# One opening block: the input loaded first, the first norm beside the bias rows' preparation, stores waited for after block 1

## The reference

```python
h = rms_norm(x, attn_norm[i])                 # block 1: x * rsqrt(mean(x*x) + 1e-6) * gain
proj = h @ w_in[i]
...
lam = (exp(sum(lambda_q1 * lambda_k1)) - exp(sum(lambda_q2 * lambda_k2)) + lambda_init)
...
bias = bias_table[:, t5_bucket(rel * dilation)]      # block 3: table (3*16 heads, 32 buckets)
...
bias = rpb[:, :, col_idx][:, row_idx]                # block 4: rpb (16 heads, 15, 31)
```

## Time and profile before

| | us |
|---|---|
| median of 3 runs (lowest, highest) | 1720.3 (1716.7, 1722.6) |
| the profiled execution | 1728.3 |
| its span, first to last instruction | 1726.2 |
| TensorE busy | 1564.6 (91%) |
| VectorE busy | 1074.9 (62%) |
| ScalarE busy | 699.1 (40%) |

### The profile page before, as it was taken

How to read it: one execution, slowest core, us unless ns; L and a number is a source line. 1 busy time by engine, 2 the same in 40 slices (tenths; PEclk the granted TensorE clock), 3 DMA queues, 4 the chain that set the end, 5 groups by cost and what they waited for, 6 DMA issues and landing times. The chain is left out here.

```text
span 1726.2 us, 28966 instructions
## 1 busy us (share of the span) xinstructions
PE 1564.6 (91%) x8809; PEld 1383.0 (80%) x8809; DVE 1074.9 (62%) x2752; ACT 699.1 (40%) x1526; POOL 5.8 (0%) x13
## 2 busy tenths in 40 slices
PE   2997789998998999999999999879999997869987
PEld 1664578887997888999999999779999997658885
DVE  3577457957997776666666666555555554266663
ACT  0343211113323443544444444346555554336552
POOL 0000000000000000000000000000000000000000
PEclk9998789999999999999999999989999999679997
DMA  6410043442224555555555555374444441075410
GB/s 246 164 38 1 2 160 111 153 153 75 92 90 142 194 191 188 194 184 182 194 184 182 194 184 183 127 261 135 151 152 137 134 139 45 1 250 165 121 26 25
DMA packets 162586, 239.33 MB, mean 139 GB/s; under 512 B 41808, under 2 KB 91472, under 8 KB 161488
## 3 DMA queue, kind: packets, MB, share of 16 engines
q1 hardware_dynamic: 162160, 238.34, 42.2%
q10 hardware_dynamic: 352, 0.07, 0.0%
HBM read 237.09 MB, written 1.28 MB: 138 GB/s over the span
## 5 line engine op out<-in xcount | busy, mean ns | idle before, releaser
L187 PE MATMUL experts_acc<-experts_uh,experts_wh 128*128 128x512 f32 x512 | 201.5, 394 | 5.7 <-DVE experts_ul L1579 5.7
L188 PE MATMUL experts_acc<-experts_ul,experts_wh 128*128 128x512 f32 x512 | 201.1, 393 | 0.0
L189 PE MATMUL experts_acc<-experts_uh,experts_wl 128*128 128x512 f32 x512 | 200.1, 391 | 0.0
L1132 PE MATMUL plain_u<-ffn_h,down_raw 128*128 128x256 f32 x832 | 192.1, 382 | 0.4 <-PEq L1217 0.4
L1552 ACT ACTIVATE experts_uh<-ffn_h 128x512 fp32r<-128x512 f32 x256 | 147.1, 624 | 83.7 <-PE experts_acc L189 79.1
L189 PE MATMUL projection<-hT_high,down_low 128*128 128x256 f32 x608 | 172.1, 283 | 0.0
L188 PE MATMUL projection<-hT_low,down_high 128*128 128x256 f32 x608 | 172.0, 283 | 0.0
L187 PE MATMUL projection<-hT_high,down_high 128*128 128x256 f32 x608 | 171.7, 282 | 0.0
L1132 PEld LDWEIGHTS plain_u<-ffn_h,down_raw 128*128 128x128 f32 x832 | 154.1, 192 | 19.5 <-issue 1.1
L1579 DVE TENSOR_TENSOR experts_ul<-ffn_h,experts_uh 128x512 fp32r<-128x512 f32 x256 | 164.7, 684 | 3.0 <-ACT experts_uh L1552 3.0
L187 PE MATMUL mix_a_pj<-mix_a_wh,hT_high 128*128 128x384 f32 x384 | 136.8, 356 | 17.0 <-DVE mix_a_wl L560 17.0
(11 more groups left out here) (274 smaller groups left out, 3014.9 us busy)
## 6 DMA issues: line engine op xcount, KB each, us to landing
down_raw<-in_downT SPq DMA_DIRECT2D x256, 256.0 KB, 3.4
ffn_h<-in_up SPq DMA_DIRECT2D x256, 256.0 KB, 2.8
mix_a_w_raw<-in_wa SPq DMA_DIRECT2D x48, 768.0 KB, 5.9
block_w_raw<-in_w SPq DMA_DIRECT2D x16, 768.0 KB, 6.6
mix_b_w_raw<-in_wb SPq DMA_DIRECT2D x16, 768.0 KB, 6.7
route_raw<-in_route SPq DMA_DIRECT2D x16, 576.0 KB, 3.7
wo<-in_wo SPq DMA_DIRECT2D x2, 2048.0 KB, 10.4
mix_a_w_raw<-in_wa SPq DMA_DIRECT2D x16, 256.0 KB, 3.3
```

Of the source, the lines that this page charges most:

```text
L187: pe.matmul(out, lhs[0], rhs[0], start=start, stop=False, skip_group_check=True)
L188: pe.matmul(out, lhs[0], rhs[1], start=False, stop=False, skip_group_check=True)
L189: return pe.matmul(out, lhs[1], rhs[0], start=False, stop=stop, skip_group_check=True)
L1132: mm = pe.matmul(self.u[b][:, 0:SEQ], self.raw[b][:, k, :], self.h[:, k, :], start=k == 0, stop=k == KD - 1, skip_group_check=True)
```

## The change

`prepare_phase` and the first `norm_phase` become one block, `opening_phase`. SP loads x first, each tile with a semaphore of its own, and the first pair's weights before the band mask; the later pairs' weights follow the constants, and two constants that only later blocks read come last. The first norm's steps are woven into the streams of the preparation: VectorE does the inverse root right after the turned table's copy, TensorE the transposes right after the one-hot product, and the lambda products stand between the second and third eviction. The seven strided copies into `staged` move from VectorE to ScalarE, the zeroing of `staged` to GpSimd. The padded table is no longer gathered in SBUF by 16 loads: SP stores a tile of zeros to `bias_pad`, and, at the start of block 1 and after a wait for that store, copies `rpb` into its place from memory to memory. The waits for the stores and for the two late constants stand at the end of SP's stream of block 1 (`finish`). `staged` and the zeros live through block 1.

```diff
 def attention_phase(nc, name, pieces, *, n_pairs, kinds, groups, hT, yT, cons, q_gain=None, k_gain=None,
-                    bias=None, load_bias=None, near=None, minus_lam=None, ahead=None):
+                    bias=None, load_bias=None, near=None, minus_lam=None, ahead=None, finish=None):
...
                 else:
                     load_piece(0, 0, 2)
                 each_pair(sp, n_pairs, one)
+            if finish is not None:
+                finish(sp)
 
...
-def prepare_phase(nc, d, sbt, scratch, ahead):
-
+def opening_phase(nc, d, sbt, scratch, pieces, gain, whole, staged, zeros, stored, pad_zeroed, late):
...
         rows = sb("rows", [3 * N_HEADS, 2 * SEQ])
-        staged = sb("staged", [3 * N_HEADS, SHIFTS, P])
-        pad = sb("pad", [N_HEADS * REL_ROWS, PAD_C])
         prod = sb("prod", [P, 2, HD])
...
+        x_in = [sem(f"x{t}") for t in range(NT)]
...
         block = c.enter_context(nc.Block())
-        loads = [(sbt[k][:], d[k]) for k in ("x", "columns")]
-        loads += [(sbt["rows"][:], d["rows"].broadcast_to([P, N_ROWS]))]
-        loads += [(sbt[k][:], d["c_" + k]) for k in ("cos", "sin", "causal", "near", "iota")]
 
         @block.sync
         def _(sp):
+            for t in range(NT):
+                sp.dma_start(x[:, t, :], d["x"][:, t, :]).then_inc(x_in[t], 16)
+            sp.dma_start(ident[:], d["c_ident"]).then_inc(ident_in, 16)
             sp.dma_start(table[:], d["t5_bias"]).then_inc(table_in, 16)
-            sp.dma_start(sbt["ident"][:], d["c_ident"]).then_inc(ident_in, 16)
             sp.dma_start(onehot[:], d["c_onehot"]).then_inc(table_in, 16)
+            sp.dma_start(sbt["columns"][:], d["columns"]).then_inc(columns_in, 16)
+            pieces.load(sp, 0, 0, 0)
             sp.dma_start(band[:], d["c_band"]).then_inc(table_in, 16)
-            for dst, src in loads:
-                sp.dma_start(dst, src).then_inc(loaded, 16)
-            ahead(sp)
+            sp.dma_start(sbt["rows"][:], d["rows"].broadcast_to([P, N_ROWS])).then_inc(loaded, 16)
+            for k in ("cos", "sin", "causal"):
+                sp.dma_start(sbt[k][:], d["c_" + k]).then_inc(loaded, 16)
+            for q in range(1, pieces.depth):
+                pieces.load(sp, q, q, 0)
+            for k in ("near", "iota"):
+                sp.dma_start(sbt[k][:], d["c_" + k]).then_inc(late, 16)
+            sp.wait_ge(blanked, 2)
+            sp.dma_start(scratch["pad"].rearrange("h r c -> (h r) c"), zeros[:]).then_inc(pad_zeroed, 16)
             sp.wait_ge(rows_ready, 1)
             sp.dma_start(scratch["rows"], staged[:]).then_inc(stored, 16)
-            sp.wait_ge(stored, 32)
-            sp.wait_ge(loaded, 16 * len(loads))
+            sp.wait_ge(loaded, 64)
+
+        @block.gpsimd
+        def _(pool):
+            pool.memset(staged[:], 0.0).then_inc(blanked, 1)
+            pool.memset(zeros[:], 0.0).then_inc(blanked, 1)
 
         @block.scalar
         def _(act):
-            act.wait_ge(zeroed, 1)
-            for h in range(N_HEADS):
-                act.dma_start(pad[h * REL_ROWS:(h + 1) * REL_ROWS, 48:48 + RPB_C],
-                              d["rpb"][h, 4:4 + REL_ROWS, :]).then_inc(rpb_in, 16)
-            act.wait_ge(rpb_in, 16 * N_HEADS)
-            act.dma_start(scratch["pad"].rearrange("h r c -> (h r) c"), pad[:]).then_inc(stored, 16)
+            act.wait_ge(x_in[1], 16)
+            act.activation(sq[:, 1, :], x[:, 1, :], ACT.Square, accum_out=ssum[:, 1:2]).then_inc(sum_ready, 1)
+            act.wait_ge(root_ready, 1)
+            act.activation(h[:, 1, :], x[:, 1, :], ACT.Copy, scale=r[:, 1:2]).then_inc(h_ready, 1)
             act.wait_ge(lsum_ready, 1)
             act.activation(lexp[:], lsum[:], ACT.Exp).then_inc(lexp_ready, 1)
-
-        @block.gpsimd
-        def _(pool):
-            pool.memset(pad[:], 0.0).then_inc(zeroed, 1)
+            act.wait_ge(blanked, 1)
+            act.wait_ge(rows_banded, 1)
+            for m in range(SHIFTS):
+                last = act.activation(staged[:, m, 0:P - 1], rows[:, m:m + RES * (P - 2) + 1:RES], ACT.Copy)
+            last.then_inc(rows_ready, 1)
 
         @block.tensor
         def _(pe):
             pe.wait_ge(ident_in, 16)
             pe.wait_ge(table_in, 48)
-            pe.transpose(pst[0:T5_BUCKETS, 0:3 * N_HEADS], table[:], sbt["ident"][0:48, 0:48]).then_inc(turned, 1)
+            pe.transpose(pst[0:T5_BUCKETS, 0:3 * N_HEADS], table[:], ident[0:48, 0:48]).then_inc(table_turned, 1)
             pe.wait_ge(tableT_ready, 1)
             pe.matmul(psr[0:3 * N_HEADS, :], tableT[:], onehot[:], start=True, stop=True).then_inc(rows_ps, 1)
+            for t in range(NT):
+                if t == 1:
+                    pe.wait_ge(h_ready, 1)
+                else:
+                    pe.wait_ge(root_ready, 2)
+                for k in range(KD):
+                    mm = pe.transpose(pt[:, 2 * t + k // 4, k % 4, :], h[:, t, k * P:(k + 1) * P], ident[:])
+                    if k % 4 == 3:
+                        mm.then_inc(turned, 1)
 
         @block.vector
         def _(dve):
-            dve.wait_ge(turned, 1)
+            dve.wait_ge(x_in[0], 16)
+            dve.tensor_tensor_reduce(sq[:, 0, :], x[:, 0, :], x[:, 0, :], 1.0, 0.0, ALU.mult, ALU.add, ssum[:, 0:1])
+            dve.drain()
+            dve.wait_ge(table_turned, 1)
             dve.tensor_copy(tableT[:], pst[0:T5_BUCKETS, 0:3 * N_HEADS]).then_inc(tableT_ready, 1)
+            dve.wait_ge(sum_ready, 1)
+            inverse_root(dve, r[:], ssum[:], D, hm[:], a[:], b_[:])
+            dve.tensor_copy(a[:], r[:]).then_inc(root_ready, 1)
+            dve.tensor_scalar(h[:, 0, :], x[:, 0, :], r[:, 0:1], None, ALU.mult).then_inc(root_ready, 1)
             dve.wait_ge(rows_ps, 1)
-            dve.memset(staged[:], 0.0)
-            dve.tensor_tensor(rows[:], psr[0:3 * N_HEADS, :], band[:], ALU.add)
-            dve.drain()
-            for m in range(SHIFTS):
-                last = dve.tensor_copy(staged[:, m, 0:P - 1], rows[:, m:m + RES * (P - 2) + 1:RES])
-            last.then_inc(rows_ready, 1)
-            dve.wait_ge(loaded, 16 * len(loads))
-            g = sbt["rows"]
-            lam0 = 4 * P
-            for i in range(2):
-                o = lam0 + 2 * i * HD
-                dve.tensor_tensor_reduce(prod[:, i, :], g[:, o:o + HD], g[:, o + HD:o + 2 * HD], 1.0, 0.0, ALU.mult,
-                                         ALU.add, lsum[:, i:i + 1])
-            dve.drain()
-
-            dve.tensor_scalar(g[:, 0:P], g[:, 0:P], HD ** -0.5, None, ALU.mult).then_inc(lsum_ready, 1)
-            dve.tensor_scalar(g[:, 2 * P:3 * P], g[:, 2 * P:3 * P], HD ** -0.5, None, ALU.mult)
+            dve.tensor_tensor(rows[:], psr[0:3 * N_HEADS, :], band[:], ALU.add).then_inc(rows_banded, 1)
+
+            dve.wait_ge(columns_in, 16)
+            for n in range(2 * NT):
+                t, k = n // 2, slice(4 * (n % 2), 4 * (n % 2) + 4)
+                dve.wait_ge(turned, n + 1)
+                dve.tensor_tensor(whole[:, k, t * P:(t + 1) * P], pt[:, n, :, :], gain[:, k].unsqueeze(2).broadcast_to([P, 4, P]),
+                                  ALU.mult)
+                if n == 1:
+                    dve.wait_ge(loaded, 64)
+                    g = sbt["rows"]
+                    lam0 = 4 * P
+                    for i in range(2):
+                        o = lam0 + 2 * i * HD
+                        dve.tensor_tensor_reduce(prod[:, i, :], g[:, o:o + HD], g[:, o + HD:o + 2 * HD], 1.0, 0.0, ALU.mult,
+                                                 ALU.add, lsum[:, i:i + 1])
+                    dve.drain()
+
+                    dve.tensor_scalar(g[:, 0:P], g[:, 0:P], HD ** -0.5, None, ALU.mult).then_inc(lsum_ready, 1)
+                    dve.tensor_scalar(g[:, 2 * P:3 * P], g[:, 2 * P:3 * P], HD ** -0.5, None, ALU.mult)
             cols = sbt["columns"]
             for k, n in (("q_a", 3), ("q_b", 1)):
...
-
-            def load_first(sp):
-                for q in range(pieces.depth):
-                    pieces.load(sp, q, q, 0)
-            prepare_phase(nc, d, sbt, scratch, load_first if start < 1 else lambda sp: None)
+            staged, zeros = sb("staged", [3 * N_HEADS, SHIFTS, P], c=c), sb("zeros", [N_HEADS * REL_ROWS, PAD_C], c=c)
+            stored, pad_zeroed, late = sem("bias_stored"), sem("pad_zeroed"), sem("late")
             if start < 1:
                 whole = sb("block1_h", [P, KD, SEQ], c=c)
-                norm_phase(nc, "norm0", x, column("attn", KD), None, sbt["ident"], whole=whole)
+                opening_phase(nc, d, sbt, scratch, pieces, column("attn", KD), whole, staged, zeros, stored, pad_zeroed, late)
                 yT = [sb(f"yT0_{n}", [P, KD, SEQ], F32R, c=c) for n in ("high", "low")]
                 wo, landed, load_wo = output_weights(c, "wo1", d["wo1"])
+
+                def store_pad(sp):
+                    load_wo(sp)
+                    sp.wait_ge(pad_zeroed, 16)
```

(34 more changed lines are left out.)

## The result

The changed kernel took 1707.8 us (1707.4 to 1711.5, four runs) against 1720.4 beside it: a ratio of 0.9934, 95% interval 0.9914 to 0.9954. That is 11 us less, between 8 and 15, or 12.7 by the medians. The forecast was 17.3. The direction and the mechanism held; the gain was a quarter to a third smaller than forecast, and the forecast's 0.990 lies outside the interval. Three executions of the later experiments took 2027 to 4023 us, with both forms of the kernel, and the medians and ratios here leave them out.

What follows compares the result with a forecast made beforehand. A 13 us hole behind a late store was taken to delay block 1, with TensorE the bound afterwards; starting block 1 at 20.05 instead of 37.30 saves 17.25 us, 1720.3 to 1703.0, range 1698 to 1709.

Steps and rivals of the forecast that it cites:

- What bounds the kernel: Opening: about 13 us without engine work, because the 168 KB rows' store stands behind block 1's weights in its queue.
- What follows moves with block 1: After the opening: TensorE is the bound, so whatever moves block 1's first product from 37.30 moves everything later by as much.
- The sign that I had named: Forecast is wrong if first product of block 1 to kernel end, 1688.9 us, grows by more than 3.
- Part 1: Order of the opening's loads: band lands at 9.85 us behind the loads ahead of it, 2.88 MB with band, at 419 GB/s.
- T: Start of TensorE's first instruction in the opening, released by band's landing; forecast at 9.95 us.
- My late bound: Band's landing in the opening at the latest: 11.8 us, with all loads at the rate of x's load, 290 GB/s.
- Part 2: Opening's chain from TensorE's first instruction to block 1: VectorE's and ScalarE's chains end together, taken as T + 10.1, at 20.05 us.
- My own sign: End of the opening: forecast is wrong if the copies into `staged` hold the block's end by more than 1 us.
- (a): Start of block 1: longer TensorE gap makes products start at the lower clock, losing 1.8 to 3.6 us; chance 0.14.
- The sum: Whole kernel: block 1 starts at 20.05 instead of 37.30, 17.25 us earlier, so 1720.3 becomes 1703.0 us.
- rival (d): Behind the opening: half-clock stretches fall elsewhere and give gain back, up to about 2 us each, 1706 to 1710; chance 0.10.
- Part 3: Moved waits for stores and the zeroed pad, in SP's stream of block 1: they cost nothing, with 40 us in hand.

Runs made afterwards that it cites:

- the early wait: Changed kernel with SP waiting for both stores behind the rpb copy at block 1's start instead of at block 1's end; 1708.4 us, one execution.
- band last: Changed kernel with the band mask's load issued behind all eight weight transfers; 1722.8 us against 1718.8 for the kernel before, ratio 1.0023.
- band first: Changed kernel with the band mask's load issued before the gain columns and the first weight pair; 1706.3 us, ratio 0.9921 to the kernel before.
- the late wait: Kernel before, with only SP's wait for the two stores moved to the end of block 1; 1706.3 us, ratio 0.9922.
- the copies first: Changed kernel with ScalarE making the seven copies into staged before it waits for the lambda sums; 1705.2 us, ratio 0.9922 to the kernel before.

## Why the prediction was right or wrong

**What bounds the kernel: right.** The hole was a wait for a store behind weights, and the store was that of the rows. Both parts have a run of their own: the wait moved alone gives 13.5 us, the store on another queue 8.2.

**What follows moves with block 1: right to within 5 us.** The rest from the first score to the last matmul was 1651 to 1664 us in four profiles of the old form and 1652 to 1659 in ten of the new one, with no relation to where block 1 began. The sign that I had named, that the distance from the first product to the end grows by more than 3 us, is split: it is 5.7 shorter than in the first profile of before and 6.8 longer than in the second, the clock's 1.7 at its start included.

**Part 1, T: wrong by 1.6 us.** I put band's landing at 9.85, and TensorE started at 11.51 instead of 9.95. The step that failed is the rate. I took 419 GB/s, measured over weights alone, for everything ahead of band. The stretches of the opening after the change:

```profile
2.00:4.65 2.65, 0.00 (x0) 0.00 (x0) 0.00 (x0) 0.03 (x1) 0.00 (x0) 1.00 0.96 295
4.65:6.10 1.45, 0.00 (x0) 0.00 (x0) 1.23 (x2) 0.00 (x0) 0.00 (x0) 1.00 1.19 394
6.10:7.10 1.00, 0.00 (x0) 0.00 (x0) 0.00 (x0) 1.00 (x2) 0.00 (x0) 1.00 0.90 338
7.10:10.80 3.70, 0.00 (x0) 0.00 (x0) 0.00 (x0) 0.15 (x2) 0.00 (x0) 1.00 1.01 370
10.80:11.40 0.60, 0.00 (x0) 0.00 (x0) 0.00 (x0) 0.00 (x0) 0.00 (x0) 1.00 0.95 318
```

The DMA engines are full almost from the start (a share of 0.9 and more), but move 295 to 394 GB/s. In 9.4 us that is 3.25 MB, so some 0.4 MB of the loads behind band had also gone in when it landed. Counted in band's own bytes, 2.88 MB in 9.4 us are 306 GB/s: 2.5 us more than my 6.9, of which 0.9 came back because the data began at 2.0 and not at 2.95. The landings place the loss. The gain columns, last ahead of the weights, landed 4.0 us after their issue at 3.08, at 7.1, where my sum has 5.8; the weights went at my rate (7.1 to 10.8, 1.57 MB); band took 0.5 instead of 0.2. So x and the small tables were too slow, not the weights; which property of these loads does it, no run shows. My late bound, 11.8, held.

**Part 2, the chain: right for VectorE, short for ScalarE.** VectorE was to end 9.75 us after T and did at 8.98 (20.49 - 11.51); the evictions and the lambda products took less than their sum. ScalarE's chain sets the end. Seven copies of 48x127, read with a stride of 4, took 2.31 us, 0.41 each, where I had taken a copy of 128x128 without a stride, 0.28, as the most. The chain was named, its end bounded at T + 10.5, and it came at T + 10.46; I chose 10.1. That is 0.35 us. My own sign, that the copies hold the block's end by more than 1 us, came true: VectorE's chain alone would have ended it at 20.8, 1.2 us earlier, and moving the copies gave back that much.

**The clock: the rival came true, 1.7 us.** I named it (a), gave it 0.14 and priced it at 1.8 to 3.6. What was wrong was the chance, and the argument against it, that the runs of the median meet it too. The gap grew from 1.05 to 3.07 us, not to the 2.4 of the forecast. The loss has two forms. In four traces (both of the changed kernel, the early wait, band last) the clock had come up at the end of the transposes or just behind them, fell again at or soon after the products' start, behind a gap of 2.9 to 3.2 us, and cost 1.6 to 1.7 (first product to first score 21.0 to 21.2 us, where full clock takes 19.5). In three (band first, the late wait, the store on ScalarE's queue, with gaps of 2.9, 1.05 and 1.05 us) it hadn't come up by the products' start, their transposes all ran at 421 ns or more, and the products were slow for 3.8 to 6.0 us: 1.9 to 3.0 lost. The other seven traces lost nothing: two of before, the copies first with its gap of 1.75 us, and the four in which TensorE was given work. So the longer gap that the forecast weighed is one half of it; whether the clock has come up by the products' start is the other, and that differed between kernels whose transposes and gap are alike (before and the late wait).

The Trainium skill ("TensorE: Matmul & The Clock Gate", Part 1) says that the throttled clock is the default and sustained activity releases it. In kind the traces agree: the same products from the same start took 17.41 us behind an idle TensorE and 15.72 behind a busy one. The two began at the same time within 0.2 us, in one profile each.

**The sum.** 17.25 - 1.6 - 0.35 = 15.3, as measured at the first product; less 1.7 for the clock, 13.6 at the first score. Against the second profile of before, whose product started at 36.5, it is 12.6 to 12.8. The medians give 12.7 and 8.5 and the ratios 11 and 9, so they lie below the traces by up to 5 us. That is rival (d), which I gave 0.10: a gain given back behind the opening, where the changed kernel's medians show a rest 1 to 5 us longer and a mean granted clock 0.003 to 0.005 lower, of which the slow 3.4 us at the start make 0.001. Band last shows it too, with some 3 us, though its block 1 starts nearly where that of before does; the old kernel with the late wait does not (about 1653 us). So it seems to go with the new form and not with the earlier start. Why, stays open.

**Part 3: right.** The moved waits cost nothing that a trace shows; SP's wait in block 1 made 10 us longer, which held a weight load for 1.8 us, changed nothing up to the first score.

## What to carry to other kernels

A wait for a store costs what stands before the store in its queue. Put the wait where its data is needed, and the first step's inputs ahead of bulk loads, one by one: a transfer of 96 KB behind 1.6 MB was worth 3.8 us here, and behind 6.3 MB of weights the whole gain. When a chain in front of TensorE is shortened, look at how long TensorE is idle just before its first dense work, and at the durations of its first records; fourteen idle transposes there gave back 1.7 us. Take a transfer's rate from a stretch with the same mix of loads, not from the bulk. And profile the old kernel twice before a difference of a few us behind the change is called noise or effect.

## What the runs showed of the hardware that I had not expected

- Full DMA engines moved 295 to 394 GB/s between 2.0 and 11.4 us and 416 to 430 later, with little but weights under way.
- TensorE came up to its upper clock at 18.6 us, did nothing from 18.9 on, and was at the lower one again at 22.0; in another kernel sixteen transposes and ten products ran at the lower clock before it came up.
- A ScalarE copy of 48x127 with a source stride of 4 took 0.41 us, one of 128x128 without a stride 0.28; the seven followed each other at 0.32.
- One program at two executions: 77 and 71 us for the same tail of block 3, at mean clocks of 0.71 and 0.80.
- Where two transfers count on one semaphore, the profile may give each the other's landing; the store on another queue showed which was which.
